# A hybrid block's MLP: second product's steps in parts of three and four behind their sets, plain sets first

## The reference, cut to what matters

```python
def sq_relu_mlp(h, w1, w2):
    return jnp.square(jax.nn.relu(h @ w1)) @ w2

def rmsnorm(x, g):
    xf = x.astype(jnp.float32)
    y = xf * lax.rsqrt(jnp.mean(xf * xf, axis=-1, keepdims=True) + EPS)
    return (y * g.astype(jnp.float32)).astype(x.dtype)

def modulate(t, g, m, i):
    return rmsnorm(t, g) * (1.0 + m[:, :, i + 1]) + m[:, :, i]
...
        x = x + mod[:, :, 5] * sq_relu_mlp(modulate(x, norm2_g[l], mod, 3), mlp_w1[l], mlp_w2[l])
```

## Time and profile before

| | |
|---|---|
| median of three runs | 2624.87 us (2621.99 to 2628.28) |
| the profiled execution | 2620.8 us, its span 2619.0 us |
| TensorE busy | 2457.4 us, 94% of the span |
| VectorE busy | 1743.4 us, 67% |
| ScalarE busy | 1050.1 us, 40% |
| GpSimd busy | 601.8 us, 23% |
| mean granted clock of TensorE | 0.977 |

### The profile page before, as it was taken

The page is one execution under the profiler, slowest core; times in us unless marked ns, Lnnn a source line. Parts: engine busy times, 40 slices in busy tenths (PEclk is TensorE's granted clock), DMA queues, the critical chain, the costliest instruction groups (busy, mean ns, idle before and its releaser), DMA issues.

```text
span 2619.0 us, 39469 instructions
## 1 busy us (share of the span) xinstructions
PE 2457.4 (94%) x14636; PEld 1353.0 (52%) x14636; DVE 1743.4 (67%) x3086; ACT 1050.1 (40%) x2078; POOL 601.8 (23%) x511
## 2 busy tenths in 40 slices
PE   7888989998899999989997899999999999999997
PEld 2445646554667868676453344444444444444443
DVE  6861545578768656556577888888896655556575
ACT  3844444366543423333454445444423322222212
POOL 0408545100000000022235443444341000000020
PEclk9999999999999999999998899999999999999999
DMA  7404323000100000130354444444527533333322
GB/s 236 132 15 140 101 85 93 18 25 9 28 19 19 17 18 18 34 106 25 79 179 141 161 165 169 141 154 156 177 80 283 200 105 98 108 101 102 99 74 65
DMA packets 176455, 260.26 MB, mean 99 GB/s; under 512 B 21320, under 2 KB 90952, under 8 KB 175608
## 3 DMA queue, kind: packets, MB, share of 16 engines
q1 hardware_dynamic: 171656, 240.95, 29.2%
q0 software_dynamic: 4608, 16.78, 2.0%
HBM read 179.18 MB, written 78.50 MB: 98 GB/s over the span
## 4 chain that ended last, share of the span: by engine, by line
PE 62%; issue 15%; DVE 11%; ACT 7%; POOL 3%; DMA 2%; SPq 0%; ACTq 0%; DVEq 0%; POOLq 0%
PE pb L2951 17%; PE pb L3050 14%; PE pb L329 12%; PE pb L2936 3%; PE pb L3065 3%; PE pb L2886 2%; DVE arena L2377 2%; DVE arena L2461 1%; PE pb L2563 1%; POOL MS L1716 1%; PE pb L338 1%; PE pb L295 1%; DVE arena L2279 1%; PE pb L2768 1%; DVE arena L2286 1%
## 5 line engine op out<-in xcount | busy, mean ns | idle before, releaser
L2951 PE MATMUL pb<-arena 128*128 128x512 f16 (+2 forms) x2760 | 594.0, 377 | 27.0 <-DVE arena L2425 16.2
L3050 PE MATMUL pb<-arena 128*128 128x512 f16 x2352 | 513.7, 379 | 4.5 <-DVE arena L2461 3.7
L2951 PEld LDWEIGHTS pb<-arena 128*128 128x128 f16 x2760 | 268.5, 99 | 347.9 <-DVE arena L2279 25.6
L329 PE MATMUL pb<-arena 128*128 128x512 f16 (+1 forms) x1944 | 413.0, 374 | 13.3 <-DVE arena L1920 4.5
L3050 PEld LDWEIGHTS pb<-arena 128*128 128x128 f16 x2352 | 229.0, 98 | 284.9 <-DVE arena L2461 12.3
L2461 DVE SCALAR_TENSOR_TENSOR arena<-pb,arena 128x512 f32<-128x512 f32 x432 | 293.0, 685 | 47.1 <-PE pb L3050 24.3
L329 PEld LDWEIGHTS pb<-arena 128*128 128x128 f16 x1944 | 191.5, 99 | 232.8 <-issue 20.2
L1545 ACT ACTIVATE pb<-pb 128x512 f32<-128x512 f32 x192 | 111.7, 582 | 202.0 <-DVE pb L2432 98.6
L338 PE MATMUL pb<-arena 128*128 128x128 f16 x2880 | 173.1, 221 | 6.8 <-ACT arena L1316 4.9
L338 PEld LDWEIGHTS pb<-arena 128*128 128x128 f16 x2880 | 168.2, 99 | 9.5 <-ACT arena L1316 5.1
L1780 POOL TENSOR_TENSOR arena<-arena 128x512 f32<-128x512 f32 x8 | 13.4, 1701 | 498.9 <-DVE arena L2461 498.9
(11 more groups left out here) (359 smaller groups left out, 3874.6 us busy)
## 6 DMA issues: line engine op xcount, KB each, us to landing
w1x<-arena SPq DMA_DIRECT2D x112, 256.0 KB, 2.1
arena<-w1x SPq DMA_DIRECT2D x112, 256.0 KB, 2.7
...
arena<-in_x SPq DMA_DIRECT2D x128, 128.0 KB, 3.9
...
```

The source lines that it names most:

```text
L329: mm = pe.matmul(pb[:, bank(jb, b), 0:n], whl[:, (i + 1) % 2, KT * ws + k, :], hT[:, k, hs, t0:t0 + n], start=(k == 0 and m == 0), stop=(k ...
L2951: mm = pe.matmul(pb[:, up_bank(pas, s, j), c], (lo if ws else hi)[:, k, :], token_op(b, L // 2, c)[:, k, hs, :], start=(k == 0 and m == 0) ...
L3050: mm = pe.matmul(pb[:, 4 + at % 4, :], left[:, hs, P * tt:P * tt + P], right[:, ws, :], start=(e == 0 and m == 0), stop=(e == 1 and m == 2))
```

## The change

The list is written anew (`phases`). Pass 0 begins with U0 U1 C0 U2 C1 U3: the plain sets are now 0 and 1 (`PLAIN`), and come last in pass 1 only (`SETS`). A step D is cut in its products 0 to 2, directly behind its second set, and 3 to 6, behind the next set. The first two sets of pass 1 (2 and 3) stand inside pass 0's last step and behind it. U's products come in the order 0, 3, 2, 1, 4, 5, 6. All sets but U0 use the same banks (`BANKS_LOW`), so a set's first product waits for the sum T1 of the set ahead. Splits of A11, A22 and A12 move from D into U; the W2 set is done in U of its own set. W2 has more stages in SBUF (three loads at once at the beginning); the act slots are 15 for 16, the W2 slots 15 for 14. The last step of a pass takes its products as 0, 2, 1, 5, 4, 3, 6, with one more sum on GpSimd and one less on VectorE inside it (`x12_joined` is done in the next set); step 0 of pass 1 takes 0, 4, 5, 1, 2, 3, 6. Token operands are fetched one by one behind the product of set 15 that used them last (`following`). The output of pass 0 is squared in pass 1's U3 and scaled there (the first pair of tiles) and in its first step (the others); its stores and the reloads of the residual move along in SyncE's queue.

The diff, cut to its core:

```diff
-        STRASSEN = 2 * NSTEP
+        PLAIN = 2
+        SETS = (tuple(range(NSET)), tuple(range(PLAIN, NSET)) + tuple(range(PLAIN)))
         PRODUCTS = ((0, 2), (4, 4), (5, 5), (1, 1), (3, 3), (2, 6), (6, 0))
-        UP_ORDER = (0, 3, 1, 2, 4, 5, 6)
+        UP_ORDER = (0, 3, 2, 1, 4, 5, 6)
...
-        BANKS_HIGH = (6, 5, 4, 7, 6, 4, 6)
...
-            return (BANKS_HIGH if s == 1 else BANKS_LOW)[j]
+            return BANKS_LOW[j]
...
-            return view(40 if x == 1 else 206, [2, 2, BLK])
+            return view({1: 40, 2: 32, 4: 40}.get(x, 206), [2, 2, BLK])
...
+            return (0, 2, 1, 3, 4, 5, 6) if s >= PLAIN else (0, 3, 1, 2)
...
-        LASTQ = (0, 5, 4, 3, 2, 1, 6)
-        def step_order(p):
-            return LASTQ if p == NSTEP - 1 else range(7)
+        LASTQ = (0, 2, 1, 5, 4, 3, 6)
...
+            return LASTQ if p == NSTEP - 1 else (0, 4, 5, 1, 2, 3, 6) if pas and p == 0 else range(7)
...
+        def phases():
+            out = [(0, "U", 0, ()), (0, "U", 1, ()), (0, "C", 0, ()), (0, "U", 2, ()), (0, "C", 1, ()), (0, "U", 3, ())]
             for pas in range(2):
                 for p in range(NSTEP):
-                    for pos, q in enumerate(step_order(p)):
-                        freed += [((pas, 2 * p + e, q), step_bank(pas, p, pos, 3) + 1) for e in range(2)]
-                for s in range(STRASSEN, NSET):
+                    more = p < NSTEP - 1
+                    out += [(pas, "D", p, (0, 1, 2)), (pas if more else 1, "U", 2 * p + 4 if more else 0 if pas else 2, ()),
+                            (pas, "D", p, (3, 4, 5, 6)), (pas if more else 1, "U", 2 * p + 5 if more else 1 if pas else 3, ())]
+            return out + [(1, "C", 0, ()), (1, "C", 1, ())]
...
-        def steps():
-            out = [("U", 0, ()), ("U", 1, ())]
-            for p in range(NSTEP - 1):
-                out += [("U", 2 * p + 2, ()), ("D", p, (0, 1, 2, 3)), ("U", 2 * p + 3, ()), ("D", p, (4, 5, 6))]
-            out += [("U", STRASSEN, ()), ("D", NSTEP - 1, tuple(range(7))), ("U", NSET - 1, ())]
-            return out + [("C", STRASSEN, ()), ("C", NSET - 1, ())]
-        A_SUMS = {(0, 1): 0, (0, 3): 1, (1, 3): 2, (2, 3): 3, (4, 1): 0, (4, 3): 1, (5, 2): 2, (6, 1): 3}
-        A_LO = {(0, 2): (0,), (1, 0): (1,), (1, 1): (2,), (1, 2): (3,), (2, 0): (4,), (2, 2): (5,), (3, 1): (6,),
-                (4, 0): (0,), (4, 2): (1,), (5, 0): (2,), (5, 1): (3,), (5, 3): (4,), (6, 0): (5,), (6, 2): (6,)}
-        A_LO_LAST = {(0, 2): (0,), (0, 3): (1,), (1, 0): (2,), (1, 2): (3,)}
+        A_SUMS = {(0, 1): 0, (0, 3): 1, (1, 1): 2, (1, 3): 3, (3, 1): 0, (3, 3): 1, (4, 1): 2, (4, 3): 3}
+        A_LO = {(0, 2): 3, (1, 0): 4, (1, 2): 5, (2, 0): 6, (3, 2): 3, (4, 0): 4, (4, 2): 5, (5, 0): 6}
+        C_SUMS = {2: 0, 4: 1, 6: 2, 8: 3}
+        C_LO = {3: 3, 5: 4, 7: 5, 9: 6}
+        C_W2 = {9: 0, 11: 1, 13: 2, 15: 3}
+        SQUARED, SQUARED_PLAIN = {0: 3, 2: 5, 1: 7}, {0: 3, 3: 5, 1: 7, 2: 9}
...
+        TILES = ((1, 3, 5, 7, 0, 2, 4, 6), PLAIN_TILES)
...
+            def following(products):
+                for j in products:
+                    fetch_tokens(PRODUCTS[j][1])
+                    fetch_w1(SETS[1][0], PRODUCTS[j][0])
...
                 for x in w1[0:2]:
                     w_hi(*x)
-                act.wait_ge(S("u_c"), uc(pas, s, "A11"))
                 squared(pas, s, "A11", 0)
+                a_hi(pas, s, 0)
+                for x in w1[2:3]:
+                    w_hi(*x)
                 for x in w2[3:4]:
                     w2_hi(*x)
-                for x in w1[2:4]:
+                for x in w1[3:4]:
                     w_hi(*x)
-                act.wait_ge(S("u_c"), uc(pas, s, "A22"))
+                if (pas, s) == (1, 3):
+                    final_sq(0, range(4))
                 squared(pas, s, "A22", 1)
+                a_hi(pas, s, a_order(s)[1])
                 for x in w2[4:5]:
                     w2_hi(*x)
-                for x in w1[4:6]:
+                for x in w1[4:5]:
                     w_hi(*x)
-                act.wait_ge(S("u_c"), uc(pas, s, "A12"))
+                for x in w2[5:6]:
+                    w2_hi(*x)
+                for x in w1[5:6]:
+                    w_hi(*x)
                 squared(pas, s, "A12", 2)
-                for x in w2[5:6]:
+                for x in w2[6:7]:
                     w2_hi(*x)
                 for x in w1[6:7]:
                     w_hi(*x)
-                for x in w2[6:7]:
-                    w2_hi(*x)
-                act.wait_ge(S("u_c"), uc(pas, s, "A21"))
+                a_hi(pas, s, 1)
                 squared(pas, s, "A21", 3)
-            def final_sq(pas):
-                for j in range(8):
-                    z = 8 * pas + j
-                    act.wait_ge(S("acc"), plain_bank(pas, NSET - 1, 2 * j + 1) + 1)
+                if (pas, s) == (1, 3):
+                    final_sq(0, range(4, 8))
...
             w1_q(1)
+            w1_r(1)
+            w1_p(1)
             pool.wait_ge(S("row_in"), 32)
             w2_scale(0)
-            w2_t1(0)
-            w1_r(1)
-            w1_p(1)
-            x_difference(0)
             w1_q(2)
             w2_scale(1)
-            for s in range(NSET - 1):
-                if s >= 2:
+            w1_r(2)
+            w1_p(2)
+            w2_scale(2)
+            w2_t1(2)
+            w1_q(3)
+            w2_t2(2)
+            w1_r(3)
+            w1_p(3)
+            w2_scale(3)
+            w2_t1(3)
+            w1_q(4)
...
                 dve.tensor_tensor(bank(3), T0, bank(3), ALU.add).then_inc(S("u_c"), 1)
+                for x in w1[0:2]:
+                    w_lo(*x)
+                a_lo(pas, s, 0)
+                for x in w1[2:3]:
+                    w_lo(*x)
                 dve.wait_ge(S("u_mm"), up_done(pas, s, 1))
                 dve.tensor_tensor(T0, T0, bank(1), ALU.add).then_inc(S("u_c"), 1)
-                for x in w1[0:2]:
-                    w_lo(*x)
-                dve.wait_ge(S("u_mm"), up_done(pas, s, 2))
                 dve.wait_ge(S("u_c"), uc(pas, s, "U2"))
                 dve.tensor_tensor(TS, T0, bank(2), ALU.add).then_inc(S("u_c"), 1)
                 for x in w2[3:4]:
                     w2_lo(*x)
-                for x in w1[2:3]:
+                for x in w1[3:4]:
                     w_lo(*x)
                 dve.wait_ge(S("u_mm"), up_done(pas, s, 4))
                 dve.wait_ge(S("u_c"), uc(pas, s, "U3"))
                 dve.tensor_tensor(a22, TS, bank(4), ALU.add).then_inc(S("u_c"), 1)
                 dve.tensor_tensor(T0, T0, bank(4), ALU.add).then_inc(S("u_c"), 1)
-                for x in w1[3:4]:
-                    w_lo(*x)
+                if (pas, s) == (1, 3):
+                    final_out(0, 0)
                 for x in w2[4:5]:
                     w2_lo(*x)
+                a_lo(pas, s, a_order(s)[1])
                 for x in w1[4:5]:
                     w_lo(*x)
+                for x in w2[5:6]:
+                    w2_lo(*x)
                 dve.wait_ge(S("u_mm"), up_done(pas, s, 5))
                 dve.tensor_tensor(a12, TS, bank(5), ALU.add).then_inc(S("u_c"), 1)
                 for x in w1[5:6]:
                     w_lo(*x)
-                for x in w2[5:6]:
+                for x in w2[6:7]:
                     w2_lo(*x)
                 dve.wait_ge(S("u_mm"), up_done(pas, s, 6))
                 dve.wait_ge(S("u_c"), uc(pas, s, "U4"))
                 dve.tensor_tensor(T1, T0, bank(6), ALU.add).then_inc(S("u_c"), 1)
                 for x in w1[6:7]:
                     w_lo(*x)
-                for x in w2[6:7]:
-                    w2_lo(*x)
+                a_lo(pas, s, 1)
...
+                            if q == 0 and tt == 0 and pas:
+                                dve.wait_ge(*late("comb", 12))
+                                dve.wait_ge(*late("comb_d", 16))
+                                dve.wait_ge(S("h_sq"), N7 + 8)
...
+                        if pas and p == 0 and 0 in qs:
+                            soon(pas, rest[1], pos, tt)
+                        else:
+                            if rest[1] >= PLAIN and (pos, tt) in A_SUMS:
+                                a_sum(*rest, A_SUMS[pos, tt])
+                            if (pos, tt) in A_LO and (rest[1] >= PLAIN or A_LO[pos, tt] == 3):
+                                a_lo(*rest, A_LO[pos, tt] if rest[1] >= PLAIN else 2)
+                        if final and pos > 2:
...
+            def soon(pas, s, pos, tt):
+                if (pos, tt) == (0, 0):
+                    a_sum(pas, s, 0)
+                    a_sum(pas, s, 1)
...
+                elif j == 0:
+                    pe.wait_ge(S("u_c"), uc(*prior, "A21"))
+                elif prior[1] < PLAIN:
+                    i = {3: 3, 1: 1, 2: 0} if prior == (0, 0) else {3: 0, 1: 3, 2: 1}
+                    pe.wait_ge(S("s_lo"), SB["lo"] + a_count(*prior, i[j]))
+                elif j == 3:
+                    pe.wait_ge(*late("a_sum", a_sums(*prior) + 3))
```

(2 more changed lines are left out.)

494 lines of the change are left out of this document (268 added, 226 removed).

## The result

The changed kernel takes 2649.5 us (median of 4 runs, 2646.1 to 2655.9) beside 2624.5 us for the kernel before (4 runs): ratio 1.0094, 95% interval 1.0079 to 1.0109. It is **0.94% slower**, 25 us, where the forecast was 2626 and the range ended at 2641. The profiled execution took 2646.1 us (span 2644.2).

The account below looks back on a forecast made before the run. It took TensorE's pauses and the half clock behind them as the bound, 38.9 us in the MLP. -20.0 + 10.7 + 2.4 + 8.2 = +1.3 us gave 2622.1 profiled, 2626.2 as median; range 2609 to 2641.

Parts of the forecast that it names:

- The start: First sets of the MLP: three pauses with half clock, 32.0 us, become one wait for T1 costing 12.0; gain 20.0.
- the walk: VectorE's queue timed operation by operation at 0.60 us each; in steady sets it put the first eviction at 23.4 us.
- The steady first half: Sets 3 to 13: late first evictions stop TensorE 0.82 us in 13 step parts, +10.7 us; the earlier 3.7 us stay.
- the forecast's own sign: First half's steady pauses: the forecast is wrong if they add up to less than 5 us or more than 20.
- Rival C: A22 stands behind a W1 split awaiting GpSimd's difference; if that ends after 12.4 us, six sets lose +15: 2641; chance 0.20.
- the sum: All terms of the whole kernel added, +1.3 us, giving 2626; own range 2617 to 2636; chance 0.46.
- The order written out for GpSimd at the start: At the MLP's start GpSimd does all of W1 first, ahead of scaling W2; part of the 20.0 us gain.
- The estimate worked out from it: Step splits in 12 parts each wait out a whole GpSimd scaling, 1.1 us more apiece, some 13 us.
- The last step: First half's last step, parts 3 to 6: 36 VectorE operations in 20.8 us make evictions late, +2.4 us (0 to 4).
- between the halves: Output squares in ScalarE's queue delay the second half's first step: 8.6 us pause plus 2.8 clock, 11.4 for 3.2.
- Fetches and the second half's steady part: Token and W1 fetches arrive in time, and the second half's steady sets have first evictions on time: no cost.
- Rival E: Short pauses at the 13 step parts lower the clock too, 2.8 us each: +36, 2663 us; chance 0.04.

Follow-up runs that it names:

- e9: e8 with the first product of set 1 in free PSUM bank 6, not bank 0, which VectorE's last sum of set 0 still reads: 2602.3 us.
- e11: The changed kernel with GpSimd's work made small as in e4 and ScalarE's fifth and seventh W2 copies ahead of its squares: 2606.4 us.
- e4: The changed kernel with GpSimd's W1 and W2 sums and scalings on 64 of 512 columns (output not the reference's): 2620.5 us.
- e3: The changed kernel with VectorE's W1 split that waits for GpSimd's difference put behind A22 and U4 again: 2635.4 us.
- e7: e6 with e5's squares, two of GpSimd's token differences in plain block 1, and set 4's W2 scaling behind step 0's first eviction: 2607.4 us.
- e6: e3 with ScalarE's copies of the fifth and seventh W2 piece also ahead of its squares of A22 and A12: 2616.5 us.
- e8: e7 with GpSimd's scalings of W2 sets 3 and 5 held until first evictions of plain block 1 and step 0's second part: 2600.7 us.
- e5: The changed kernel with the first half's eight output squares placed in ScalarE's gaps inside set 3 of the second half: 2644.5 us.
- e10: e9 with VectorE's split for the second product of the second half's first step ahead of the third sum and third eviction: 2600.9 us.

## Why the forecast was wrong

**The start** (a gain of 20.0 forecast, 17.3 measured): one pause for T1 of 10.35 us and not 9.1, with 2.7 us of half clock, and 0.72 for U4, 0.5 for an eviction, which the walk did not have. Right in mechanism; e9 shows that its reason was only the first of two.

**The steady first half** is the step that failed, as a size. The walk itself was good: its 23.4 us is 23.75 in the trace, and with GpSimd made small its 10.7 us come out as 14.1, which e11 then takes to zero by the very copies that the walk waited for. By the forecast's own sign, more than 20 us of steady pauses, it was wrong: behind its start the first half has 34 us of them, without their slow matmuls. What was missing is the other term. I wrote that the 3.7 us of before, "mostly one VectorE operation that GpSimd's scaling of W2 lengthens", stay. They became some 23 us (39.8 less the 17.0 that e4 leaves), for three reasons, each seen in a trace. The second and the third were undone by themselves or nearly so (e3; e7 beside e6); the first only together with them, in e4:

- The prices of 0.60 in the walk are those of a set in which GpSimd's sums lie beside hardly any split. In the sets behind a three-product part they lie beside five splits or six, and the queue, which had 0.4 us to spare before, now has less than none. A lengthening that cost little became a pause at full price.
- Rival C came in part. In the set at 1670.30, behind a four-product part, the difference ends 10.8 us in, exactly as expected; in the set at 1705.23, behind a three-product part, 12.8 (12.4 was the point), and A22 and the first eviction are 1.65 us later than in the other sets, not 2.5. I held C against the sum as an alternative at 0.20; it is one of its terms.
- The order written out for GpSimd at the start was counted at the start only. The four differences and the scaling of set 4 that the extra stage lets go ahead fall beside set 3: 9.1 us at step 0 and the half clock in it. The forecast did not walk GpSimd's queue through sets 2 to 4.

**Shared access.** The trace showed 1.15 to 2.09 us for lengthened splits before; here it goes to 2.87 for one and 5.59 for two. The Trainium skill (SBUF — State Buffer, "SBUF: two separate sides") has a lock held for a whole instruction against a VectorE operation with two SBUF inputs; this case agrees, with 2.87 us for a split beside a scaling of 2.3 (e8) and 0.68 for its neighbours with one input in PSUM; 2.87 is about that scaling and the split's own 0.6. The estimate worked out from it, some 13 us more, was set beside the sum and not into it; it would have given 2639.

**The last step** (2.4, measured 1.9) and **between the halves** (11.4, measured 10.8: a pause of 8.86 for 8.6 and a half clock of 1.8 for 2.8): right, with the place, the releaser and the squares ahead of it. The eight operations that it put behind the squares (4.9 us) are what leaves e5 its pause.

**Fetches and the second half's steady part**, costed at nothing: no wait in either, as forecast.

**Rival E** (short pauses lower the clock): the clock of the stretch at 1700 is 1.00 with pauses of 0.67 and 1.93 us in it. Right to give it little for pauses that short; e10's 2.31 us did lower the clock.
